# Two of the five first transfers of a two-block transformer kernel issued by ScalarE instead of the sync engine

## The chip, the cores and the metric

The kernel runs on one core of one Trainium2 chip. The metric is the device time of one execution in microseconds (us); lower is better. The time before is the median of three runs.

## The reference

Two different transformer blocks run one after the other on x, which is 256 positions by 1024 features in float32. The first block has a gated recurrent branch, an attention branch and a feed-forward part of width 2816. The second has a sliding-window branch, a latent attention branch and another feed-forward part. What matters here is the very first step, an RMS norm followed by the first projection:

```python
h = rmsnorm(x, norm1_g[l])
u = jnp.einsum('bsd,de->bse', h, w_in[l])          # w_in: 1024 x 7168
x_rnn, g_rnn, q, k, v, g_br = jnp.split(u, list(cuts), axis=-1)
xa = causal_dwconv(x_rnn, conv_w[l], conv_b[l])
```

## The kernel before

**Tiling.** Features lie on the 128 partitions, so x is 8 chunks of 128 features by 256 positions. Every weight matrix is cut into slabs of 128 by 2048 float32 values (1 MB), 132 slabs in all; from slab 2 on they go round a ring of three buffers (raw0 to raw2). ScalarE (ACT) rounds each slab to a high part (whi), VectorE (DVE) subtracts to get the low part (wlo), and TensorE (PE) makes each product from three matmuls (high by high, high by low, low by high). The activations are split in the same way (ahi, alo). Each engine has its own hand-written program; semaphores order them.

**The start.** The first two slabs and x don't use the ring. They are packed by the host into one array "first", a row of 192 parameter columns and then 8 chunks, each of 256 columns of x and 512 columns of weights. It comes in five pieces (FIRST_PIECES, L80), each with a semaphore of its own (first_in[0] to first_in[4]):

- piece 0: the parameters and chunk 0, 960 columns, 480 KB
- piece 1: chunk 1, 768 columns, 384 KB
- pieces 2, 3 and 4: chunks 2 and 3, 4 and 5, 6 and 7, 1536 columns and 768 KB each

The sync engine (SP) issues all five (L477 to L479), then two halves of slab 2 (L482), then slabs 3 and 4 (L459). Slab 5 waits there until DVE is done with slab 2.

**What uses the pieces.** ACT does for each chunk k a norm_hi (L538, ahi) and a hi_part (L621, whi); after chunks 3 and 5 it also squares two chunks of x for the norm (L542), and after chunk 7 two more pairs of them, each followed by one half of slab 2. DVE does for each chunk a norm_lo (L965, alo) and a lo_part (L1051, wlo), and then the two halves of slab 2 (L1051). PE runs 11 warm-up matmuls (L1863), then first_pair (L1841 to L1859): 12 matmuls for each chunk in three groups of four (L1848, L1852, L1855), each group behind the semaphore of its operands. Then it takes slab 2 (L1540 to L1542), whose second half waits for all of the first three low parts. GpSimd (POOL) adds the squares up (L1456).

Before its first chunk ACT waits for a semaphore of DVE (consts) and computes one small square root (L618), for which a table is loaded; then it waits for first_in[0].

Of the kernel before, what the change touches and what calls it, by code (L numbers as in the profile page):

```python
# [79 lines left out]
FIRST_PIECES = ((0, 1), (1, 2), (2, 4), (4, 6), (6, 8))  # L80
FIRST_PIECE_OF = (0, 1, 2, 2, 3, 3, 4, 4)
HEAD, CHUNK = 192, SEQ + 2 * WIDE
# [38 lines left out]
def slab_columns(s):  # L121

    if PLAN[s][1] == "strip":
        return 4 * strip_width(s)
    return 3 * QLAT if PLAN[s][1] == "rows3" else SLAB
# [61 lines left out]
def emptied(g):  # L187

    who = GROUPS[g][2]
    return who, sum(1 for x in GROUPS[:g + 1] if x[2] == who)  # L190
# [41 lines left out]
def pair(p):  # L232

    return HEADS + p + 1


def program(nc, t):
    f32, f32r = mybir.dt.float32, mybir.dt.float32r
    ALU, ACT, AX = mybir.AluOpType, mybir.ActivationFunctionType, mybir.AxisListType.X
    with ExitStack() as ctx:  # L240
        def sb(name, shape, dt=f32):
            return ctx.enter_context(nc.sbuf_tensor(name, shape, dt))

        def sem(name):
            return ctx.enter_context(nc.semaphore(name))
# [5 lines left out]
        FIRST = sb("first", [P, HEAD + KD * CHUNK])  # L251
# [125 lines left out]
        first_in = [sem(f"first_in{i}") for i in range(len(FIRST_PIECES) + 2)]  # L377
# [41 lines left out]
        def used_value(s):  # L419

            if s == S_XR:
                return first_used, 1
            base = FFN2 if s >= FFN2 else FFN1
            if base <= s < base + 3 * STEPS:
                i = s - base
                n0 = 0 if base == FFN1 else STEPS
                if i < 2:
                    return group_done, GROUP_OF[(base, 0)] + i + 1
                j, kind = divmod(i - 2, 3)
                if i == 3 * STEPS - 1 or kind == 2:  # L430
                    if i == 3 * STEPS - 1:
                        return down_bank, 4 if n0 == 0 else 8
                    return down_used, n0 // STEPS * (STEPS - 1) + j + 1
                return group_done, GROUP_OF[(base, 0)] + 2 * (j + 1) + kind + 1
            return group_done, max(g for (x, _), g in GROUP_OF.items() if x == s) + 1

        def x_value(n, c):
# [4 lines left out]
                return x_ready, c // 2 + 1  # L442
            return bank_free["dve"], emptied(GROUP_OF[((S_OUT if n == 1 else S2_OUT) + c // 2, 0)])[1]

        def raw_value(s):

            return 16 * (s // RING)


        @block.sync  # L450
        def _(sp_eng):
            e = sp_eng

            def load(s):

                if s >= RING + 2:
                    e.wait_ge(lo_ready, s - RING + 1)
                n = slab_columns(s)
                e.dma_start(raw[s % RING][:, 0:n], t["slabs"][s][:, 0:n]).then_inc(raw_in[s % RING], 16)  # L459

            def load_at(s, slot):

                e.wait_ge(lo_ready, s - RING + 1)
                e.dma_start(raw[slot][:, :], t["slabs"][bass.ds(s, 1)].rearrange("o p n -> p (o n)")).then_inc(
                    raw_in[slot], 16)

            def ffn(base, then=None):
                load(base)
                load(base + 1)
                if then:  # L470
                    then()
                with e.Fori(1, STEPS) as j:
                    for i in range(3):
                        load_at(j * 3 + (base - 1 + i), (base + 2 + i) % RING)
                load(base + 3 * STEPS - 1)

            for i, (c0, c1) in enumerate(FIRST_PIECES):  # L477
                cols = slice(HEAD + CHUNK * c0 if c0 else 0, HEAD + CHUNK * c1)
                e.dma_start(FIRST[:, cols], t["first"][:, cols]).then_inc(first_in[i], 16)  # L479
            for i in range(2):  # L480
                cols = slice(1024 * i, 1024 * i + 1024)
                e.dma_start(raw[2][:, cols], t["slabs"][2][:, cols]).then_inc(first_in[len(FIRST_PIECES) + i], 16)  # L482
            for s in range(RING, 2 * RING):
                load(s)
            e.dma_start(ident[:, :], t["ident"]).then_inc(in_misc, 16)
            e.dma_start(masks[:, :, :], t["masks"]).then_inc(in_misc, 16)
            for c in range(2):
                e.dma_start(ropeA[:, c], t["rope_a"][c].rearrange("(h p) d -> p h d", p=P)).then_inc(in_misc, 16)
                e.dma_start(ropeB[:, c], t["rope_b"][c].rearrange("(h p) d -> p h d", p=P)).then_inc(in_misc, 16)
            e.dma_start(rowt[:, :], t["swa_sinks_2"]).then_inc(in_misc, 16)  # L490
            for s in range(2 * RING, FFN1):
                load(s)
            ffn(FFN1)
            for s in range(S2_SEQ, FFN2):
                load(s)

            def gains():
                e.wait_ge(m_lo, 8)
                e.dma_start(fing, t["final_norm_g"].rearrange("(a n) -> a n", a=1).to_broadcast([P, D])).then_inc(
                    in_fing, 16)  # L500

            ffn(FFN2, gains)
            for i, (h, c) in enumerate(((0, 0), (0, 1), (1, 1))):
                e.wait_ge(y_ready, i + 1)
                e.dma_start(t["out"][0][P * h:P * h + P, 512 * c:512 * c + 512],
                            outp[:, h, 512 * c:512 * c + 512]).then_inc(out_done, 16)
            e.wait_ge(out_done, 16 * 2 * HALVES)
# [3 lines left out]
        def _(e):  # L511
# [15 lines left out]
            def pre(s):  # L527
                if s < SLABS:
                    hi(s % RING, raw_value(s), used_value(s - RING) if s >= RING else None)
# [74 lines left out]
            def pair_exp(p):  # L604

                e.wait_ge(aM, pair(p))
                x = soft[p % 2]
                for i in range(2):
                    for h, cols in ((0, slice(0, P)), (1, slice(P, 3 * P))):
                        ins = e.activation(x[:, i, cols], x[:, i, cols], ACT.Exp, bias=nb2[:, i, h:h + 1],  # L610
                                           scale=(64 if p < 4 else MLA_D) ** -0.5,
                                           accum_out=sums2[:, i, h:h + 1])
                if p < 4:
                    ins = e.activation(esink2[:, :, :], zs2[:, :, :], ACT.Exp)
                ins.then_inc(aE, 1)

            e.wait_ge(consts, 1)
            e.activation(finr[:, 0:1], epst[:, :], ACT.Sqrt)  # L618
# [10 lines left out]
            for i in range(2):  # L629
                squares(0, 2 + i)  # L630
                cols = slice(1024 * i, 1024 * i + 1024)
# [28 lines left out]
            for s in range(S_G, S_RI):  # L660
                if s == S_G + 2:
                    pre(s + 3)
                i = s - S_G
# [51 lines left out]
            for s in range(S_Q, S_GATE):  # L715
                pre(s + 3)
                which, i = divmod(s - S_Q, 4)
# [33 lines left out]
            for s in range(S_GATE, FFN1):  # L751
# [11 lines left out]
                if s >= S_OUT:  # L763
                    i = s - S_OUT
# [8 lines left out]
            def ffn(which, base, n0, func):  # L773
# [35 lines left out]
                def hi_at(j, off):  # L809


                    used = (down_used, j + n0 // STEPS * (STEPS - 1)) if off == 4 else (group_done, j * 2 + (g_up + off - 1))
                    hi((base + off) % RING, j * 16 + raw_value(base + off), used)
# [51 lines left out]
            for s in range(S2_GA, FFN2):  # L865
# [7 lines left out]
                if s == S2_UKV:  # L873
                    pair_exp(PAIR_S[S2_UQ + 1 - S2_GA])
                    kv_evac(1)
                    pre(s + 2)
# [20 lines left out]
                if scores is not None and s != S2_UQ + 1:  # L897
                    pair_exp(scores)
# [8 lines left out]
                if s >= S2_OUT:  # L907
                    i = s - S2_OUT
# [30 lines left out]
        def _(e):  # L939
# [430 lines left out]

            for s in range(S2_GA, FFN2):
                _, _, scores, _, values = pairs_at(s)
                normal = PAIR_N.get(s - S2_GA)
                if values is not None:
# [162 lines left out]
        def _(e):  # L1537
# [187 lines left out]
            def pairs_first(s):  # L1725

                turn, _, _, _, values = pairs_at(s)
                if turn is not None:
                    pair_turn(turn)
                if values is not None:  # L1730
                    pair_values(values)
# [354 lines left out]
```

## Time and profile before

| what | value |
|---|---|
| median of three runs | 797.68 us (797.62 to 798.31) |
| profiled execution, its own time | 797.33 us |
| its span, first to last instruction | 795.5 us |
| granted TensorE clock, mean | 0.999 |
| PE busy | 787.8 us, 99% of the span |
| DVE, ACT, POOL busy | 73%, 57%, 9% |

The profile is of one execution. Times within it are counted from the first instruction; the 1.8 us between the span and the execution's own time lie around it. "Busy" is time in which an engine had an instruction in hand. A row of the timeline gives start, duration, engine, line, operation, what it writes and reads, and in brackets how long the engine had been idle and what released it.

### The profile page before, as it was taken

Reading aid. Unit: us, or ns where it says so; the run is one execution under the profiler, and the core shown is the slowest. Engines: PE = TensorE matmul, PEld = TensorE weight load, DVE = VectorE, ACT = ScalarE, POOL = GpSimd, SP = SyncE. Lnnn points to the kernel's source line nnn. Section 1 sums busy time; section 2 is a strip of 40 time slices with the busy share of each in tenths; the row PEclk is TensorE's granted clock in tenths of the full one; section 3 lists DMA queues with packets and bytes.
Section 4 is the critical chain, followed back from the end, with each engine's and each line's share of the span. In section 5 each row is a group of like instructions: output and inputs, shape, how many; then the busy total and the mean of one; then the engine's idle time right before and its main releaser. Section 6 shows DMA issues by size and latency. Waiting matters only on the chain.

```text
span 795.5 us, 12020 instructions
## 1 busy us (share of the span) xinstructions
PE 787.8 (99%) x4622; PEld 690.9 (87%) x4622; DVE 582.8 (73%) x705; ACT 453.3 (57%) x594; POOL 75.0 (9%) x92
## 2 busy tenths in 40 slices
PE   8999999999999999999999999999999999999997
PEld 8998888888889899999999897888799888888886
DVE  7986897566577898777787877766878766666664
ACT  7679765666345654544454658767455544454444
POOL 2220231000002000000000532410003000000000
PEclk9999999999999999999999999999999999999999
DMA  8645555443545454555454552444345545455521
GB/s 322 243 161 203 183 192 213 158 159 133 184 159 210 156 205 171 178 194 208 163 206 158 183 197 87 156 159 150 139 155 213 196 181 185 184 198 176 206 105 53
DMA packets 21718, 140.88 MB, mean 177 GB/s; under 512 B 3378, under 2 KB 3506, under 8 KB 5682
## 3 DMA queue, kind: packets, MB, share of 16 engines
q1 hardware_dynamic: 21538, 140.13, 48.9%
q8 instruction: 24, 0.39, 0.2%
q10 hardware_dynamic: 144, 0.26, 0.1%
q14 instruction: 12, 0.10, 0.0%
HBM read 139.33 MB, written 1.05 MB: 176 GB/s over the span
## 4 chain that ended last, share of the span: by engine, by line
PE 97%; DVE 1%; ACT 1%; DMA 1%; issue 0%; SPq 0%; DVEq 0%
PE pp L1577 21%; PE pp L1540 20%; PE pp L1542 20%; PE pp L1541 20%; PE pp L1579 10%; PE pp L1695 1%; PE pp L1721 1%; PE pp L1708 1%; DMA first<-in_first 1%; PE pp L1684 1%; DVE wlo L1051 1%; PE pp L1758 0%; PE pp L1630 0%; PE pp L1642 0%; PE pp L1658 0%; PE pp L1650 0%
## 5 line engine op out<-in xcount | busy, mean ns | idle before, releaser
L950 DVE TENSOR_TENSOR wlo<-raw,whi 128x2048 fp32r<-128x2048 f32 x129 | 298.2, 2314 | 96.2 <-ACT whi L525 95.9
L525 ACT ACTIVATE whi<-raw 128x2048 fp32r<-128x2048 f32 x129 | 246.4, 1911 | 101.2 <-PE pp L1542 101.1
L1577 PE MATMUL pp<-ahilo,whi 128*128 128x512 f32 x704 | 221.4, 396 | 0.0
L1540 PE MATMUL pp<-whi,ahi 128*128 128x512 f32 (+2 forms) x412 | 162.8, 395 | 0.0
L1542 PE MATMUL pp<-whi,alo 128*128 128x512 f32 (+2 forms) x412 | 159.4, 387 | 0.0
L1579 PEld LDWEIGHTS pp<-ahilo,wlo 128*128 128x128 f32 x704 | 132.2, 188 | 31.2
L1541 PE MATMUL pp<-wlo,ahi 128*128 128x512 f32 (+2 forms) x412 | 159.2, 386 | 0.0
L1579 PE MATMUL pp<-ahilo,wlo 128*128 128x256 f32 x704 | 138.3, 278 | 0.0
L1540 PE MATMUL pp<-ahi,whi 128*128 128x256 f32 x416 | 118.5, 285 | 1.4 <-DVE wlo L1051 1.4
L1542 PE MATMUL pp<-ahi,wlo 128*128 128x256 f32 x416 | 117.7, 283 | 0.0
L1541 PE MATMUL pp<-alo,whi 128*128 128x256 f32 x416 | 117.7, 283 | 0.0
L1577 PEld LDWEIGHTS pp<-ahilo,whi 128*128 128x128 f32 x704 | 108.0, 189 | 0.8
L780 ACT ACTIVATE qk<-pp 128x512 f32<-128x512 f32 x44 | 26.3, 598 | 120.0 <-PE pp L1579 120.0
L1542 PEld LDWEIGHTS pp<-whi,alo 128*128 128x128 f32 x412 | 77.3, 188 | 15.6
L1540 PEld LDWEIGHTS pp<-whi,ahi 128*128 128x128 f32 x412 | 77.4, 188 | 15.1 <-issue 0.9
L1541 PEld LDWEIGHTS pp<-wlo,ahi 128*128 128x128 f32 x412 | 77.5, 188 | 13.8
L1540 PEld LDWEIGHTS pp<-ahi,whi 128*128 128x128 f32 x416 | 79.8, 192 | 2.0 <-DVE wlo L1051 1.6
L1541 PEld LDWEIGHTS pp<-alo,whi 128*128 128x128 f32 x416 | 79.8, 192 | 0.1
L1542 PEld LDWEIGHTS pp<-ahi,wlo 128*128 128x128 f32 x416 | 79.8, 192 | 0.0
L1456 POOL TENSOR_TENSOR vv<-vv 128x512 f32<-128x512 f32 x12 | 24.5, 2040 | 408.5 <-ACT vv L542 408.1
L1252 DVE TENSOR_TENSOR qk<-pp,qk 128x512 f32<-128x512 f32 x44 | 30.3, 689 | 36.9 <-ACT qk L780 36.9
L1540 PE MATMUL pp<-whi,ahilo 128*128 128x512 f32 x64 | 25.7, 402 | 0.0
(238 smaller groups left out, 780.7 us busy)
## 6 DMA issues: line engine op xcount, KB each, us to landing
raw<-in_slabs SPq DMA_DIRECT2D x125, 1024.0 KB, 4.8
first<-in_first SPq DMA_DIRECT2D x3, 768.0 KB, 6.9
raw<-in_slabs SPq DMA_DIRECT2D x2, 832.0 KB, 4.4
raw<-in_slabs SPq DMA_DIRECT2D x2, 576.0 KB, 3.7
raw<-in_slabs SPq DMA_DIRECT2D x2, 512.0 KB, 9.9
out<-gg SPq DMA_DIRECT2D x3, 256.0 KB, 2.1
xa<-in_final_norm_g SPq DMA_DIRECT2D x1, 512.0 KB, 6.5
first<-in_first SPq DMA_DIRECT2D x1, 480.0 KB, 3.5
```

The costliest lines, as they stand in the source:

```text
L525: e.activation(whi[slot][:, :], raw[slot][:, :], ACT.Copy).then_inc(hi_ready, 1)
L780: e.activation(dst, banks[:, :, SEQ:2 * SEQ], ACT.Copy).then_inc(f_cross, 1)
L950: e.tensor_tensor(wlo[slot][:, :], raw[slot][:, :], whi[slot][:, :].bitcast(f32), ALU.subtract).then_inc(lo_ready, 1)
L1051: e.tensor_tensor(wlo[slot][:, cols], src, whi[slot][:, cols].bitcast(f32), ALU.subtract).then_inc(lo_ready if done else first_lo, 1)
L1252: return e.tensor_tensor(dst, banks[:, :, 0:SEQ], dst, ALU.add)
L1456: ins = e.tensor_tensor(SQ[:, 0:2, :], SQ[:, 0:2, :], SQ[:, 2 * i:2 * i + 2, :], ALU.add)
L1540: e.matmul(out, lhs[0], rhs[0], start=first, stop=False, skip_group_check=True)
L1541: e.matmul(out, lhs[0], rhs[1], start=False, stop=False, skip_group_check=True)
L1542: return e.matmul(out, lhs[1], rhs[0], start=False, stop=last, skip_group_check=True)
L1577: e.matmul(out[:, m, :], w[m][0], ACT2[:, k, :], start=k == 0, stop=False, skip_group_check=True)
L1579: ins = e.matmul(out[:, m, 0:SEQ], w[m][1], ACT2[:, k, 0:SEQ], start=False, stop=k == KD - 1, skip_group_check=True)
L1684: ins = e.transpose(PST2[0:P if p < 4 else MLA_D, n, o:o + P], src, ident[:, :])
```

## The change

Pieces 1 and 3 are now issued by ScalarE, at the top of its program, before its wait for consts and its first activation. Pieces 0, 2 and 4 are issued by the sync engine, as before and in that order. Sizes, addresses and semaphores of the five pieces stay. The sync engine's later transfers follow behind three issues instead of five. The columns of a piece are now computed in a small function.

```diff
+        def first_columns(i):
+
+            c0, c1 = FIRST_PIECES[i]
+            return slice(HEAD + CHUNK * c0 if c0 else 0, HEAD + CHUNK * c1)
+
...
-            for i, (c0, c1) in enumerate(FIRST_PIECES):
-                cols = slice(HEAD + CHUNK * c0 if c0 else 0, HEAD + CHUNK * c1)
-                e.dma_start(FIRST[:, cols], t["first"][:, cols]).then_inc(first_in[i], 16)
+            for i in (0, 2, 4):
+                e.dma_start(FIRST[:, first_columns(i)], t["first"][:, first_columns(i)]).then_inc(first_in[i], 16)
             for i in range(2):
                 cols = slice(1024 * i, 1024 * i + 1024)
                 e.dma_start(raw[2][:, cols], t["slabs"][2][:, cols]).then_inc(first_in[len(FIRST_PIECES) + i], 16)
...
                 ins.then_inc(aE, 1)
+
+            for i in (1, 3):
+                e.dma_start(FIRST[:, first_columns(i)], t["first"][:, first_columns(i)]).then_inc(first_in[i], 16)
 
             e.wait_ge(consts, 1)
             e.activation(finr[:, 0:1], epst[:, :], ACT.Sqrt)
```

## Rows read from the trace of the kernel before

**Rows 1.** The page: busy time of the engines, and the last chain.

```profile
PE 787.8 (99%) x4622; PEld 690.9 (87%) x4622; DVE 582.8 (73%) x705; ACT 453.3 (57%) x594; POOL 75.0 (9%) x92
...
PE 97%; DVE 1%; ACT 1%; DMA 1%; issue 0%; SPq 0%; DVEq 0%
```

**Rows 2.** Waits of PE over the whole span: total us, times, longest.

```profile
PE pp L1540 <- DVE wlo L1051: 1.4, 1, 1.4
PE pp L1863 <- DVE ones L1046: 1.1, 1, 1.1
```

**Rows 3.** The chain of waits in order of time, 0 to 26 us.

```profile
1.65 5.48 DMA first<-in_first
...
12.48 0.88 DVE alo L965
...
14.70 3.95 DVE wlo L1051 x2
18.70 0.39 PE pp L1540
```

**Rows 4.** Timeline of ACT, 0 to 22 us.

```profile
0.73 1.28 ACT L618 ACT_TABLE_LOAD   x1 [0.73 <-PEq L2072]
2.03 0.20 ACT L618 ACTIVATE finr<-epst 128x1 f32<-128x1 f32 x1
4.36 0.51 ACT L538 ACTIVATE ahi<-first 128x256 fp32r<-128x256 f32 x1 [2.12 <-DMA first<-in_first]
...
5.29 0.50 ACT L538 ACTIVATE ahi<-first 128x256 fp32r<-128x256 f32 x1
...
7.15 0.51 ACT L538 ACTIVATE ahi<-first 128x256 fp32r<-128x256 f32 x1 [0.84 <-DMA first<-in_first]
...
9.52 0.50 ACT L538 ACTIVATE ahi<-first 128x256 fp32r<-128x256 f32 x1
```

**Rows 5.** DMA issues of L479: pieces 0, 1, 2 and 4 each alone, then three together.

```profile
first<-in_first SPq DMA_DIRECT2D x1, 480.0 KB, 3.5
...
first<-in_first SPq DMA_DIRECT2D x1, 384.0 KB, 4.1
...
first<-in_first SPq DMA_DIRECT2D x1, 768.0 KB, 5.5
...
first<-in_first SPq DMA_DIRECT2D x1, 768.0 KB, 8.3
...
first<-in_first SPq DMA_DIRECT2D x3, 768.0 KB, 6.9
```

**Rows 6.** The sync engine's queue, 0 to 25 us: start, duration.

```profile
0.73 2.35 SPq L479 DMA_DIRECT2D first<-in_first  x5
```

**Rows 7.** Windows of the start: busy time, PE clock, DMA share, GB/s.

```profile
1.50:2.50 1.00, 1.00 (x6) 1.00 (x6) 0.00 (x0) 0.72 (x2) 0.00 (x0) 1.00 0.83 104
2.50:3.50 1.00, 1.00 (x7) 1.00 (x6) 0.00 (x0) 0.00 (x0) 0.00 (x0) 1.00 0.91 358
3.50:5.50 2.00, 2.00 (x13) 1.91 (x13) 0.50 (x2) 1.15 (x3) 0.61 (x3) 1.00 1.04 424
...
17.30:18.70 1.40, 0.00 (x0) 0.00 (x1) 1.40 (x2) 1.27 (x1) 0.26 (x1) 1.00 0.57 228
```

**Rows 8.** The DMA queue's packets and bytes, 0 to 20 us.

```profile
q1 hardware_dynamic: 1296, 6.39, 82.3%
```

**Rows 9.** DMA issues at the end: two output tiles earlier, then one from each queue.

```profile
out<-gg SPq DMA_DIRECT2D x2, 256.0 KB, 2.1
...
out<-gg ACTq DMA_DIRECT2D x1, 256.0 KB, 2.5
out<-gg SPq DMA_DIRECT2D x1, 256.0 KB, 2.7
```

**Rows 10.** Timeline of the end, both queues.

```profile
792.42 0.40 ACTq L935 DMA_DIRECT2D out<-gg  x1
792.45 0.33 SPq L505 DMA_DIRECT2D out<-gg  x1
```

## The prediction

> **What bounds the kernel now.** The first view is the page: PE is busy 99% of the span and the chain that ended last is 97% PE [rows 1]. So a change outside PE's work can count only where PE waits. The waits of PE come second: in the whole span there are two, 1.1 us before its first instruction and 1.4 us for a low part of the first slabs, before the matmul at 18.70 us [rows 2]. From 18.70 us to its last matmul PE waits for no one that the view lists. Whatever moves 18.70 moves the end by the same amount, and nothing later gives it back, since what follows is relative to PE and to the engines it releases.
>
> The third view is the chain of waits at the start. Read it backwards: PE at 18.70 comes behind DVE's work from 12.48 on, and that behind ACT's, which the transfer issued at 1.65 released after 5.48 us [rows 3]. That transfer is piece 2. The timeline of ACT says the same: it stands idle for 2.12 us until piece 0 and for 0.84 us until piece 2, and never again [rows 4]. So 18.70 hangs on when piece 2 lands, through an unbroken ACT and then DVE.
>
> The landing times follow from issue and time to landing [rows 5]. The sync engine issues one piece each 0.47 us (five in 2.35 us from 0.73 us) [rows 6], so at about 0.73, 1.18, 1.65, 2.12 and 2.59.
>
> - Piece 0: 0.73 + 3.5 = 4.2. ACT starts at 4.36.
> - Piece 1: 1.18 + 4.1 = 5.3. ACT needs it at 5.29, just in time.
> - Piece 2: 1.65 + 5.5 = 7.1. ACT needs it 0.84 before 7.15, at 6.3, and waits.
> - Piece 3: of the three large ones the middle value is 6.9, and it is this one: 2.12 + 6.9 = 9.0. ACT needs it at 9.52.
> - Piece 4: 2.59 + 8.3 = 10.9. ACT needs it two chunks and a squaring after 9.52, at about 11.9.
>
> From one landing to the next it is 1.0, 1.9, 1.9 and 1.9 us for 384 and three times 768 KB, about 400 GB/s and more, and the windows show 424 GB/s from 3.5 us on [rows 7]. The pieces are limited by what the DMA engines move, not by when they are issued. The order in which the bytes arrive is what counts, and one queue gives exactly the order in which ACT wants them.
>
> **The change part by part.** (a) Two issues leave the sync engine, two are added on ACT. Each costs the issuing queue about 0.4 us (0.40 on ACT at the end of the kernel, [rows 10]). On ACT they stand ahead of the table load and the small square root, 0.73 to 2.23 us [rows 4]; those move by 0.9 us and end at about 3.1. They are hidden under the wait for piece 0, which has 2.12 us. Without that cover they would cost the 0.9. Cost 0.
>
> (b) Piece 2 is issued at 1.18 instead of 1.65, piece 4 at 1.65, and the slab loads 0.94 us earlier. If issue were the limit, this would be a gain of 0.47 us at piece 2. Since the DMA engines are full, issue alone gains nothing but in the ramp: 104 GB/s in the window to 2.5 us and 358 in the next [rows 7]. If a second queue lifts the 358 to 424, that is 66 KB, 0.16 us. This is the most likely size; the end of the range is that the whole 0.47 us is gained.
>
> (c) The order of bytes. Two queues now have work at the same time on the same DMA engines. I read how they share from the end of the kernel, where both queues issue 256 KB within 0.03 us [rows 10]: alone such a transfer lands after 2.1 us, together they need 2.5 and 2.7 [rows 9]. 256 KB at 424 GB/s are 0.62 us. If one went first, it would still need 2.1 and the other 2.7. If they alternate finely, both need 2.7. The two were slowed by 0.4 and 0.6, so it is close to fine alternation.
>
> How many turns each takes: nine transfers land or nearly land in the first 20 us, and 1296 packets are 9 times 144, that is 128 rows and 16 more [rows 8]. A row of a piece is then one packet whatever its length, and pieces 0 and 1 have the same number of packets, as have pieces 2 and 3. Alternating packet by packet, piece 0 ends with piece 1, when 864 KB are moved: at the old landing of piece 1, 5.3 us, 1.0 later than now. Then piece 2 alternates with piece 3 and both end when 2400 KB are moved: at the old landing of piece 3, 9.0 us, instead of 7.1. Piece 4 still lands at 10.9, and the slabs behind it where they did, or after what ACT needs.
>
> The Trainium skill (DMA: Bandwidth & Descriptors, "Queues, rings and completion order") says that each DMA engine takes turns between the queues it has work for, a packet at a time, and that a packet is typically 9 to 17 descriptors. The first half agrees with the slowdown of 0.4 and 0.6 us at the end. By the second half a turn could be a whole piece's share of an engine, and then piece 0 could pass as before: the sum would be 0 instead of 1.7, the first rival below.
>
> (d) From the landing to PE. Chunk 0 on ACT starts at about 5.3, chunk 1 follows without a wait and ends at 7.2, so ACT waits again until piece 2, to 9.0 instead of 7.15: +1.87 us at most. Against it stand 0.16 of the ramp and up to 0.23 if piece 2's last packets (98 KB over the 16 engines, at 424 GB/s) go ahead of piece 3's, so 1.5 to 1.87. I take 1.7, near the middle. From there ACT and DVE run exactly as they did; POOL's additions are released by ACT's squares and move along. PE itself starts 1.0 later and at chunk 2 1.7 later; its own work before the wait ends at 17.3 now [rows 7] and would at 19.0, before the DVE release at 20.4. Its extra idle stretches are each about 1 us, shorter than the 1.4 us at 17.30 to 18.70, over which the granted clock stayed 1.00 [rows 7], so no clock loss.
>
> Sum: 0 + 1.7 (ramp and order of the last packets already in it) = +1.7 us. On the profiled execution, 797.33 us, this gives 799.0; on the median, which is 0.35 higher, 799.4. With PE never waiting afterwards, the whole of it stays. What can be told from no change in this kernel is about 0.2%, 1.6 us. So I forecast slower, only just.
>
> **The rivals.**
>
> - **The pieces pass in whole turns, or first come first served (not slower).** If an engine finishes its eight rows of piece 0 before it turns to piece 1, and those of piece 2 before piece 3, the order is 0, 1, 2, 3, 4 as now. The sum is then between 0 and the gain in (b): 797.2 to 797.7, no change. It decides if piece 0 still lands at 4.2. For it: the sync engine and ACT start level, and piece 2 is issued just beside piece 3. Against it: at the end of the kernel neither transfer landed after 2.1 us. The Trainium skill (DMA: Bandwidth & Descriptors, "Issuing engines are not separate DMA queues") states that a second issuing engine saves only the time to initiate; read alone, that is this case, and it doesn't speak of what order does to the first piece.
> - **The table load runs ahead of ACT's issues.** It started at 0.73 us, before consts could be ready, so it isn't behind that wait [rows 4]; it could also be ahead of the two transfers. They would then be issued at about 2.0 and 2.5. Piece 0 lands as before. Piece 1 starts when piece 2 does and shares with it: both land at 7.1, and ACT waits for piece 1 (needed at 5.29) and is 0.9 late at chunk 2. Piece 3 shares with piece 4 and lands at 10.9 instead of 9.0; ACT needs it at 9.5 + 0.9 and in fact starts chunk 4 at 10.9 instead of 9.52: +1.4 us, 799.1, within 0.2%. Against it: the load carries the line of the activation, and other loads stand next to theirs.
> - **A gain.** The most that any earlier landing of piece 2 can give is ACT's wait of 0.84 us, 796.8, which is within 0.2%. To be faster by more, piece 0 would have to land earlier too by about another us, and with it the first issue doesn't move. I know no mechanism.
> - **Worse than summed.** The two sequencers delay each other's issues by one issue time, 0.4 to 0.5 us, and the pieces share as forecast: +2.2, 799.9.
>
> **How the numbers follow.** The forecast, fine alternation, 0.62. It gives +1.4 to +1.9, for which about three of four lie above 1.6. Whole turns or first come, 0.15, no change. Table load first, 0.13, +1.4, nearly all within 0.2%. Worse, 0.07, slower. A gain that can be measured, 0.03 for what I don't see. Slower: 0.62 times three quarters is 0.47, with 0.07 from the last and a trifle from the others, 0.55. Within 0.2%: the other 0.15 of the forecast, 0.15 and 0.12, 0.42. Faster 0.03. The range leaves out the whole turns and the unseen gain, and reaches from a share that costs only half, +0.6, over both orders to the sum of the worse case with 0.1 for spread: 798.3 to 800.0.
>
> **What the profile would show.** Chain: still piece 2, ACT, DVE, PE. ACT's queue: two issues at 0.73 and about 1.15, then the table load. Piece 0 to landing 4.5 us instead of 3.5, ACT's first chunk at 5.3 instead of 4.36. ACT's chunk 2 at about 8.9 instead of 7.15, and no wait after it. PE's one wait for DVE at about 20.4, and from there the distance to the end as before, 776.8 us. GB/s the same from 3.5 us on. Wrong would be: piece 0 at 4.2 (whole turns), the load at 0.73 with issues behind it, a wait of ACT at chunk 1 or 4, or a span that doesn't move by what chunk 2 moves, in which case something after 18.70 had slack that I didn't see.

## The result, and the profile after

The changed kernel takes 799.12 us by median (798.87 to 799.34, 20 runs); the kernel before, in 20 runs, 797.6 us (797.28 to 798.38). The ratio is 1.0019, with a 95% interval of 1.0013 to 1.0025: slower, by 1.5 us. The interval doesn't hold 1, but the ratio lies a hair under the 0.2% at which I put the border to "no change". The forecast was 799.4, with a range of 798.3 to 800.0. Three executions of the experiments below lay far above all others (972 and 1309 us with piece 1 alone, 4477 us with the late issues) and are left out of the ratios; they move no median by more than 0.02 us. The profiled execution took 799.17 us, its span is 797.4 us, 1.9 more than before.

The page of the changed kernel, busy time of the engines. PE's work is the same to a tenth of a microsecond as in [rows 1]; the difference lies in waits.

```profile
PE 787.8 (99%) x4622; PEld 690.8 (87%) x4622; DVE 583.0 (73%) x705; ACT 453.3 (57%) x594; POOL 75.0 (9%) x92
```

The timeline of ACT of the changed kernel, against [rows 4]. (Lines after the new helper are 4 to 7 higher: L538 is now L542, L618 is L625.)

```profile
0.74 0.90 ACTq L622 DMA_DIRECT2D first<-in_first  x2
1.66 1.28 ACT L625 ACT_TABLE_LOAD   x1 [1.66 <-PEq L2079]
2.96 0.20 ACT L625 ACTIVATE finr<-epst 128x1 f32<-128x1 f32 x1
5.37 0.51 ACT L542 ACTIVATE ahi<-first 128x256 fp32r<-128x256 f32 x1 [2.21 <-DMA first<-in_first]
...
6.31 0.49 ACT L542 ACTIVATE ahi<-first 128x256 fp32r<-128x256 f32 x1
...
8.95 0.51 ACT L542 ACTIVATE ahi<-first 128x256 fp32r<-128x256 f32 x1 [1.62 <-DMA first<-in_first]
...
11.32 0.49 ACT L542 ACTIVATE ahi<-first 128x256 fp32r<-128x256 f32 x1
```

The issues come first, the table load behind them, and both end long before piece 0. The first chunk starts at 5.37 instead of 4.36 us, the third at 8.95 instead of 7.15, and from there every start is 1.80 later: 11.32 against 9.52.

The DMA issues of the changed kernel, each piece alone, with time to landing, against [rows 5]: piece 0, piece 1, piece 2, piece 3 (ACT) and piece 4.

```profile
first<-in_first SPq DMA_DIRECT2D x1, 480.0 KB, 4.6
first<-in_first ACTq DMA_DIRECT2D x1, 384.0 KB, 4.8
...
first<-in_first SPq DMA_DIRECT2D x1, 768.0 KB, 7.7
...
first<-in_first ACTq DMA_DIRECT2D x1, 768.0 KB, 8.2
first<-in_first SPq DMA_DIRECT2D x1, 768.0 KB, 9.4
```

With issues at 0.73, 0.74, 1.18, about 1.2 and 1.65 us they land at 5.3, 5.5, 8.9, 9.4 and 11.0. Before, they landed at 4.2, 5.3, 7.1, 9.0 and 10.9. Pieces 1, 3 and 4 are 0.1 to 0.4 behind where they were; pieces 0 and 2 have been slowed to meet them. Piece 2 was even issued 0.47 us earlier.

How finely the queues share can be counted. The profile has one packet for each row of a piece. These are the packets of the sync engine's queue (q1) and of ScalarE's (q10) in the changed kernel between 3 and 4 us, when only pieces 0 and 1 are on their way: packets, MB, share of the 16 DMA engines' time.

```profile
q1 hardware_dynamic: 58, 0.22, 55.5%
q10 hardware_dynamic: 60, 0.18, 46.7%
```

A piece lands in 16 parts, each adding one to its semaphore. In the trace of the changed kernel the parts of piece 0 come between 4.66 and 5.29 us and those of piece 1 between 4.85 and 5.50; before, those of piece 0 came between 3.69 and 4.26. If each DMA engine had finished its share of one piece before it took up the other, in whichever order, one of the two pieces would have had a part landed there by about 4.3. None had.

The chain of waits of the changed kernel, against [rows 3], and PE's waits over the whole span, against [rows 2].

```profile
1.18 7.75 DMA first<-in_first
8.95 0.51 ACT ahi L542
...
14.29 0.88 DVE alo L972
...
16.51 3.94 DVE wlo L1058 x2
20.49 0.38 PE pp L1547
```

```profile
PE pp L1855 <- ACT whi L628: 1.7, 2, 1.2
PE pp L1547 <- DVE wlo L1058: 1.5, 1, 1.5
PE pp L1870 <- DVE ones L1053: 1.1, 1, 1.1
```

Every link is the old one, 1.8 us later: DVE at 14.29 (12.48), PE at 20.49 (18.70). PE has a new wait of 1.7 us in two parts, ahead of chunks 0 and 2, and keeps its wait of 1.5 for DVE. From 20.49 to the end of the span are 776.9 us; before it was 776.8. Nothing was given back.

Last, the windows of the start, busy time, PE clock, DMA share and GB/s, against [rows 7].

```profile
1.50:2.50 1.00, 1.00 (x6) 1.00 (x6) 0.00 (x0) 0.84 (x1) 0.00 (x0) 1.00 0.75 80
2.50:3.50 1.00, 1.00 (x7) 1.00 (x6) 0.00 (x0) 0.65 (x2) 0.00 (x0) 1.00 0.94 345
3.50:5.50 2.00, 1.85 (x13) 1.66 (x12) 0.00 (x0) 0.13 (x1) 0.14 (x1) 1.00 1.04 424
```

The rate is the same 424 GB/s, and the ramp is no faster with two queues than with one: 80 and 345 where it was 104 and 358. Over all profiles of this document the first two windows have 88 to 108 and 337 to 358 GB/s where all pieces come from one queue and ScalarE issues nothing, and 80 to 101 and 299 to 349 where the pieces come from two.

### The profile page after: what moved, and what is told of

It reads as the page before. It is cut to its first block, busy times and chain, and to the rows that moved or that the text cites. A ratio compares the mean times of both kernels' runs of the same rounds, so it can differ in the third digit from the quotient of the medians.

```text
span 797.4 us, 12020 instructions
## 1 busy us (share of the span) xinstructions
PE 787.8 (99%) x4622; PEld 690.8 (87%) x4622; DVE 583.0 (73%) x705; ACT 453.3 (57%) x594; POOL 75.0 (9%) x92
## 4 chain that ended last, share of the span: by engine, by line
PE 97%; DMA 1%; DVE 1%; ACT 1%; issue 0%; SPq 0%; DVEq 0%
PE pp L1584 21%; PE pp L1547 20%; PE pp L1549 20%; PE pp L1548 20%; PE pp L1586 10%; PE pp L1702 1%; DMA first<-in_first 1%; PE pp L1728 1%; PE pp L1715 1%; PE pp L1691 1%; DVE wlo L1058 1%; PE pp L1765 0%; PE pp L1637 0%; PE pp L1649 0%; PE pp L1665 0%; PE pp L1657 0%
```

## The experiments

Each experiment was timed beside the kernel before on the same chip. The kernel before took 797.36 us beside the runs with piece 3, with piece 1, with the late issues and the first with eight pieces; 797.49 beside eight pieces on two queues, the two small loads and the changed kernel again; 797.51 beside piece 4, six pieces and the second run with eight. Differences below are to that median.

**Piece 3 alone from ACT.** This tells whether the queues share by rows or by bytes, and whether the number of issues on ACT matters.

```diff
-            for i in (0, 2, 4):          # sync engine
+            for i in (0, 1, 2, 4):
-            for i in (1, 3):             # ScalarE
+            for i in (3,):
```

> Only piece 3 is issued by ScalarE; pieces 0, 1, 2 and 4 stay with the sync engine. Theory (two queues take turns a row at a time, so a piece ends when its own rows and as many rows of the other queue are moved): piece 0 now shares with piece 3, whose rows are twice as long as those of piece 1, and ends after 480 + 768 = 1248 KB, so it lands at about 6.2 us, later than in the changed kernel (5.33). Piece 1 follows at about 7.1 and piece 2 at 9.0; ScalarE's third chunk starts at about 9.0, as in the changed kernel, and the whole is again +1.8 us to the kernel before, about 799.2. Rival A (the queues share by bytes, not by rows): piece 0 ends after 960 KB, at 5.5 us; the rest as in the theory. Rival B (what costs is the work of issuing on ScalarE): one issue in place of two, so about +0.8.

Measured: 799.44 us, +2.1, ratio 1.0024 (1.0015 to 1.0034). Timeline of ACT of this kernel:

```profile
6.24 0.51 ACT L542 ACTIVATE ahi<-first 128x256 fp32r<-128x256 f32 x1 [3.57 <-DMA first<-in_first]
...
7.38 0.51 ACT L542 ACTIVATE ahi<-first 128x256 fp32r<-128x256 f32 x1
...
9.27 0.51 ACT L542 ACTIVATE ahi<-first 128x256 fp32r<-128x256 f32 x1 [0.86 <-DMA first<-in_first]
```

Piece 0 landed 5.4 us after its issue at 0.73, at 6.1. By rows it was to be 6.2, by bytes 5.5. The packets from 3 to 5 us, with pieces 0 (q1) and 3 (q10) on their way, say the same: as many rows, but more bytes for the queue whose rows are longer.

```profile
q10 hardware_dynamic: 82, 0.50, 60.8%
q1 hardware_dynamic: 81, 0.31, 38.6%
```

So the queues share by rows, long or short. Rival B is gone: one issue on ACT cost as much as two and a little more. Though ACT started 0.9 us later than in the changed kernel, the third chunk is only 0.3 later (9.27, where about 9.0 was expected). The whole follows the third chunk.

**Piece 4 alone from ACT.** The same edit with pieces 0 to 3 on the sync engine.

> Only piece 4, the last that is wanted, is issued by ScalarE at the top; pieces 0 to 3 stay with the sync engine. Theory (what is sent ahead shares with what is wanted first, whichever it is): piece 4 shares with piece 0, so piece 0 lands at 6.2, piece 1 at 7.1, piece 2 at 9.0, piece 3 at 10.9, all as in the run with piece 3 alone: ScalarE's third chunk starts at 9.0 to 9.3 and the whole is +1.8 to +2.1 us, 799.3. Rival (the harm came from piece 3 overtaking by its place in the order, since ScalarE wants it next after piece 2): clearly less, +1 or below.

Measured: 799.41 us, +1.9, ratio 1.0024 (1.0014 to 1.0034). ACT's first chunk started at 6.16 and its third at 9.20 us. The last piece wanted, issued at the top of the second queue, does the same harm as piece 3: it took its turns with piece 0.

**Piece 1 alone from ACT.** Pieces 0, 2, 3 and 4 stay with the sync engine.

> Only piece 1 is issued by ScalarE; pieces 0, 2, 3 and 4 stay with the sync engine. Theory: pieces 0 and 1 share and both land at about 5.3 us, so ScalarE and TensorE start 1.0 us late as in the changed kernel, but piece 2 has no one to share with and lands at 7.1 us as before. ScalarE, through with two chunks at 7.2, starts its third at 7.2 instead of 7.15: the whole is +0.1 us, no change that can be told. Rival (what costs is the late start of the first chunk, or the use of a second queue as such): +1.0 us or more, 798.6.

Measured: 797.47 us, +0.1, ratio 1.0 (0.9991 to 1.001). Timeline of ACT:

```profile
0.74 0.41 ACTq L622 DMA_DIRECT2D first<-in_first  x1
...
5.25 0.51 ACT L542 ACTIVATE ahi<-first 128x256 fp32r<-128x256 f32 x1 [2.57 <-DMA first<-in_first]
...
7.15 0.51 ACT L542 ACTIVATE ahi<-first 128x256 fp32r<-128x256 f32 x1
```

This is the experiment that separates the two delays of the change. The first chunk is 0.9 us late, as in the changed kernel, and it costs nothing, since the time is taken from the wait ahead of the third, which starts at 7.15 to the hundredth as before. The change differs from this run only in piece 3, so its whole cost is piece 3 beside piece 2.

**Eight pieces of one chunk, on two queues.** Four issues on each engine.

```diff
-FIRST_PIECES = ((0, 1), (1, 2), (2, 4), (4, 6), (6, 8))
-FIRST_PIECE_OF = (0, 1, 2, 2, 3, 3, 4, 4)
+FIRST_PIECES = tuple((i, i + 1) for i in range(8))
+FIRST_PIECE_OF = tuple(range(8))
...
+            for i in (0, 2, 4, 6):       # sync engine
...
+            for i in (1, 3, 5, 7):       # ScalarE
```

> Eight pieces of one chunk each, the even ones issued by the sync engine, the odd ones by ScalarE (four issues ahead of its table load). Theory: the two queues share as in the changed kernel, but now only neighbours of 384 KB share: pieces 0 and 1 land at 5.3 us, 2 and 3 at 7.1, 4 and 5 at 9.0, 6 and 7 at 10.9. ScalarE starts at 5.35, has its third chunk at 7.2 and no wait worth naming after it: +0.1 us to the kernel before, 797.7, although four issues and two queues are used. Rival (two queues or issues on ScalarE cost by themselves): as much as the changed kernel or more, +1.5 to +2.5.

Measured: 797.35 us, -0.1, ratio 0.9999 (0.999 to 1.0008). Timeline of ACT:

```profile
0.74 2.23 ACTq L622 DMA_DIRECT2D first<-in_first  x4
2.99 1.28 ACT L625 ACT_TABLE_LOAD   x1 [2.99 <-issue]
...
5.30 0.51 ACT L542 ACTIVATE ahi<-first 128x256 fp32r<-128x256 f32 x1 [0.81 <-DMA first<-in_first]
...
7.16 0.49 ACT L542 ACTIVATE ahi<-first 128x256 fp32r<-128x256 f32 x1
```

Two queues and twice the issues on ACT cost nothing that shows when only neighbours share and a neighbour is small. Of the cover that hid the table load 0.81 us was left.

**Two small loads on ACT instead of pieces.** The load of the sink values and the second ropeB load were moved from the sync engine to the top of ACT's program; all five pieces stay with the sync engine.

> The kernel before, with two small loads (the 8 sink values and one rope table of 16 KB) moved from the sync engine to the top of ScalarE's program; all five pieces stay with the sync engine. It puts two issues ahead of the table load without bytes that matter. Theory: the table load starts at about 1.6 instead of 0.73 us, hidden under the wait for piece 0; piece 0 lands at 4.3 to 4.4; the whole is within 0.2 us of before. Rival (the two issues on ScalarE are the cost): +0.9 to +1.8 us.

Measured: 797.56 us, +0.1, ratio 1.0 (0.9991 to 1.0009). The table load ran from 1.75 us, the first chunk started at 4.43. Issue work on ACT by itself costs nothing that shows here.

**Pieces 1 and 3 from ACT, but behind its first activation.** The loop over (1, 3) stands after the wait for consts and the square root.

> Pieces 1 and 3 are issued by ScalarE as in the changed kernel, but behind its table load and first activation, at about 2.2 us. Theory: piece 0 is nearly alone and lands at 4.2 to 4.4 us as before; piece 1 shares with piece 2, both land at about 7.1, so ScalarE's second chunk starts at 7.1 instead of 5.29 and its third at 8.1; piece 3 shares with piece 4 and lands at about 10.9, where ScalarE wants it at 10.4: its fifth chunk starts at 10.9 instead of 9.52. The whole is +1.4 us, about 799.0. Rival (in the changed kernel it is the delay of piece 0 that costs, so with it gone the cost goes): +0.2 or less.

Measured: 798.34 us, +1.0, ratio 1.001 (1.0001 to 1.0019). Its profiled execution took 798.71 us. Timeline of ACT:

```profile
0.73 1.28 ACT L622 ACT_TABLE_LOAD   x1 [0.73 <-PEq L2078]
1.12 0.90 ACTq L624 DMA_DIRECT2D first<-in_first  x2
...
4.49 0.51 ACT L542 ACTIVATE ahi<-first 128x256 fp32r<-128x256 f32 x1 [2.26 <-DMA first<-in_first]
...
7.01 0.51 ACT L542 ACTIVATE ahi<-first 128x256 fp32r<-128x256 f32 x1 [1.50 <-DMA first<-in_first]
...
10.77 0.51 ACT L542 ACTIVATE ahi<-first 128x256 fp32r<-128x256 f32 x1 [0.32 <-DMA first<-in_first]
```

The start of the first, second and fifth chunk are within 0.15 us of what was expected, and the rival falls: piece 0 is in time again and a cost stays. By the profile it is 1.25 us (10.77 against 9.52) and by the median 1.0, where 1.4 was expected. The interval of the ratio alone, from 1.0001, would not rule out the rival's 0.2 us; the timeline does. But the premise about the issue was wrong: I took 2.2 us, and the trace has them at 1.12, while the table load still runs. This is taken up at the end.

**The changed kernel again.**

> The changed kernel once more, beside the runs above on the same chip: both theories say what was measured, about +1.5 us to the kernel before.

Measured: 799.15 us, +1.7, ratio 1.0021 (1.0012 to 1.003). ACT's third chunk started at 9.03 us in this profile.

**Can the wait for piece 2 be had?** ScalarE's wait of 0.84 us before its third chunk would be the gain. Three runs with all pieces on the sync engine: eight pieces of one chunk, twice, and six pieces, with only piece 2 cut in two, FIRST_PIECES = ((0, 1), (1, 2), (2, 3), (3, 4), (4, 6), (6, 8)).

> The kernel before with the array cut into eight pieces of one chunk each, all issued by the sync engine: the same bytes in the same order. Theory (PE's resumption at 18.70 us hangs on when chunk 2 lands, and on nothing later): chunk 2 lands at 6.2 instead of 7.1 us, ScalarE's wait of 0.84 us goes, and the whole gains 0.8 us, about 796.8; chunks 3 to 7 land each about 0.93 us later than the one before and are in time. Rival (the chain has a second limit close behind the transfer, TensorE's own rate or the next piece): a gain of 0.2 us or less, or a loss by three more issues.

> The eight pieces from the sync engine once more, for a second look at chunk 3, which landed at 8.2 us instead of 7.1 in its first profile while the DMA rate fell to 307 GB/s around 6 us. Theory A (the many small pieces make it slow each time): chunk 3 is late again and the whole gains 0.3 us as before. Theory B (that gap belongs to the one execution): chunk 3 lands at 7.1 to 7.3, the third chunk starts at 6.3 and the gain by median is the same 0.3 to 0.8 us.

> The kernel before with only piece 2 cut in two (chunks 2 and 3 each a piece of 384 KB), all six from the sync engine. Theory (ScalarE's wait for chunk 2 is what can be had, and the next piece is the second limit): chunk 2 lands at 6.2 us and starts at 6.3, chunk 3 at 7.2, and the piece of chunks 4 and 5 lands at 9.0, where ScalarE now wants it at 8.7: 0.3 of the 0.84 us is given back there, and the whole gains 0.5 us, 796.9. Rival (as in the eight pieces, a chunk alone can land a full microsecond late): a gain of 0.3 us or less, with the wait at chunk 3.

Measured: eight pieces 797.08 and 797.24 us, both -0.3, ratios 0.9995 (0.9986 to 1.0004) and 0.9997 (0.9988 to 1.0006); six pieces 797.43 us, -0.1, ratio 0.9999 (0.999 to 1.0008). Each interval holds 1, so no gain is shown, where 0.8 was expected of the first and 0.5 of the six pieces. The two rows are ACT's fourth chunk in the first and in the second run of the eight pieces:

```profile
8.26 0.51 ACT L538 ACTIVATE ahi<-first 128x256 fp32r<-128x256 f32 x1 [0.84 <-DMA first<-in_first]
```

```profile
7.53 0.51 ACT L538 ACTIVATE ahi<-first 128x256 fp32r<-128x256 f32 x1 [0.37 <-DMA first<-in_first]
```

With eight pieces the third chunk starts at 6.40 and 6.14 us, as hoped, and the wait moved to the fourth. With six pieces it starts at 6.83, after a wait of 0.47, and waits of 0.15 and 0.32 follow at the fourth and fifth, together more than the old 0.84. In all three the DMA rate dips in the window from 5.5 to 6.5 us: 307 and 338 GB/s, and 341 with six pieces, where the kernel before has 436. These are that window in the first run, the second run and the run with six pieces.

```profile
5.50:6.50 1.00, 1.00 (x10) 1.00 (x9) 1.00 (x3) 1.00 (x4) 0.00 (x0) 1.00 0.94 307
```

```profile
5.50:6.50 1.00, 1.00 (x7) 1.00 (x6) 1.00 (x3) 1.00 (x3) 0.00 (x0) 1.00 0.93 338
```

```profile
5.50:6.50 1.00, 1.00 (x10) 0.94 (x9) 1.00 (x4) 0.86 (x2) 0.00 (x0) 1.00 1.04 341
```

So theory B of the second run falls: the dip is there in all three profiles, though its size varies and chunk 3 came at 7.5 us in the second, nearer to B's 7.1 to 7.3 than to the 8.2 of the first. With eight pieces on two queues the same window has 421 GB/s. In the packets the dip is a few rows that take long: a row of a one-chunk piece takes 121 ns as a rule, and in the first run two that began between 5.5 and 6.0 us took 840 and 885 ns. A chunk must wait for the last of its 16 parts, and those of chunk 3 came from 6.75 to 8.24 us in that run, a spread of 1.5 us where piece 2 has 0.6 in the kernel before. I have no cause for the long rows. In the second run there was also another limit: PE had no wait for DVE left. Its first group of four took 1.20 us (0.71 in the kernel before's timeline), it worked without a gap to 18.15, and the matmul that stood at 18.70 came at 18.16. So this execution could gain about half a microsecond and no more, as its span, 795.0 us, shows. That isn't a bound for all executions: in this trace PE's matmul records start 0.21 us apart up to about 7.2 us and 0.12 after that, and in the kernel before the close spacing begins at about 4.9, with a granted clock of 1.00 in both. The fastest execution of this run took 796.57 us, 0.9 under the median beside it. What sets the moment of the faster pace wasn't examined.

```profile
17.51 0.64 PE L1855 MATMUL pp<-ahi,wlo 128*128 128x256 f32 x4
18.16 0.39 PE L1540 MATMUL pp<-ahi,whi 128*128 128x256 f32 x1
```

None of the ten experiments is clearly faster than the kernel before.

## Why the prediction was right

**What bounds the kernel: right.** One wait of PE at 18.70 us, hanging on piece 2, and no slack behind it. The third chunk moved by 1.80 us, PE's resumption by 1.79 and the rest of the span by 0.1.

**(a), issues and table load hidden on ACT: right.** The order was the one expected, the square root ended at 3.16, and the run with two small loads there gave +0.1.

**(b), the ramp: wrong, and small.** I gave 0.16 us for a faster ramp, with no row for it. The windows show none; two queues started no faster than one.

**(c), the sharing: right, and the main term.** Piece 0 was put at 5.3 and landed at 5.3; piece 2 at 9.0 less the two small gains, 8.8, and landed at 8.9. That packets, not bytes, are taken in turn was read from a count of packets alone; the run with piece 3 alone tells it apart (6.1 against 5.5 us, and 81 rows to 82). What I had from the end of the kernel, 2.5 and 2.7 us against 2.1, was enough for the sign. The Trainium skill (DMA: Bandwidth & Descriptors, "Queues, rings and completion order") has an engine take turns between queues a packet at a time, a packet being typically 9 to 17 descriptors. The trace agrees with the turns. It doesn't show turns of that size: counted in rows, 9 are more than the 8 that a DMA engine has of a piece if its 128 rows are spread evenly over 16 engines, so one of pieces 0 and 1 would have passed whole, and no part of either landed before 4.66 us. With issues level the first rival is out.

**(d), from landing to PE: right in mechanism, 0.1 us small.** I took 1.7, the profile has 1.8. Of the two deductions the ramp did not come; the last packets' order did, in part: piece 2 landed 0.5 us ahead of piece 3, of which 0.4 lies in piece 3 being later than before. No clock was lost: after its new idle stretch of 1.19 us PE's first group of four took 0.71 us as before, and the granted clock is 1.00 in every window.

**The sum: 1.7 forecast, 1.5 by the medians of 20 runs, 1.7 in the second measurement.** The profiled executions differ by 1.84 (799.17 and 797.33), so the sum itself was 0.1 small, as in (d). The profiled one of before lies near the low end of its 20 runs (797.28 to 798.38), so the step from one execution to the median hid a part. That the medians came out nearer to the forecast than to "no change" rests on the mechanism; on which side of 0.2% they fell, it could not tell, and I had given "no change" 0.42. Why the kernel before varies more than the changed one (798.87 to 799.34) wasn't examined; that piece 1 and piece 2 land just around when they are wanted in the one and not in the other is a guess.

**The rivals.** Whole turns: no, by the landing of pieces 0 and 1 and by the packets. Table load first: no, by its row at 1.66 us. The run with late issues comes near to what that rival had put together, later issues of pieces 1 and 3: +1.0 to +1.25, where the rival had +1.4. A gain: none. Delayed issues: the issues stood where they were forecast.

What was not separated in the forecast is that the delay of piece 0 by itself is free. It followed from the arithmetic, since ACT waited in any case at chunk 2, and the run with piece 1 alone shows it: +0.1.

## What to carry to other kernels

When the chain of waits begins with a transfer, ask first whether it is late by its issue or by the bytes ahead of it. Here, with the DMA rate already level at 424 GB/s, a second issuing queue brought no byte sooner; it only let later transfers take turns with the one that was awaited, and a transfer with as many rows then landed when both were done. If a second queue is wanted all the same, make the pieces small and alternate neighbours, so that what overtakes is wanted next anyway (that cost nothing here, and gained nothing), and look at how much cover the issuing engine has left for its own start.

## What the runs showed that I had not expected

- An issue on ACT does not wait for the table load ahead of it: in the late run the load runs from 0.73 to 2.01 us and the small square root from 2.03, both ahead in the program, and the two issues are recorded from 1.12, just when consts had come.
- Issued level (0.73 and 0.74 us), piece 1 took turns with piece 0 and piece 0 landed at 5.3. Recorded as issued at 1.12, it let piece 0 land at 4.4 (3.7 us after its issue) and landed itself at 7.0. The packets say what happened: in the changed kernel ScalarE's queue moved its first row at 2.40 us, 1.7 after the issue; in the late run at 3.48, 2.4 after it, when the first DMA engine was about through with piece 0 (its first part landed at 3.79; in the kernel before, where one queue keeps the order, the same two times are 3.37 and 3.69). Between 3.0 and 3.45 us the changed kernel moved 24 rows for the sync engine's queue and 25 for ScalarE's; the late run has this line alone:

```profile
q1 hardware_dynamic: 44, 0.17, 92.0%
```

  So the two transfers hardly shared. Whether each DMA engine had taken up piece 0 as a whole, or the second queue started late for a reason of its own, stays open.
- With more and smaller pieces on one queue the DMA rate fell to between 307 and 341 GB/s for the microsecond from 5.5 us, in all three profiles; on two queues it didn't (421). Single rows took up to 0.9 us in two of the three. The cause stays open.
